# Attention stage of a streaming encoder: the low parts of the gated weights, subtracted on POOL for every unit

## What is computed

```
u = rms_norm(h, g_mix);  z = u @ w_in
q, k, v, a, b = split(z)               # 8 heads x 64; a and b are 512 wide
glu = a * sigmoid(b)                   # "gated" columns: the last 1024 of w_in
att = band_attend(rms_norm(q), rms_norm(k), v, rel_bias)   # own chunk of 64 and 8 before it
cv  = silu(layer_norm(depthwise_conv31(glu) + conv_b))
h   = h + concat(att, cv) @ w_out      # then a SwiGLU block and a gated embedding
```

## Time and profile before

| what | before |
|---|---|
| median of 3 runs | 2595.4 us (2593.06 to 2597.45) |
| profiled execution | 2595.5 us; its span 2593.7 us, 1.8 us around it |
| granted TensorE clock, mean | 0.999 |
| busy share PE / DVE / ACT / POOL | 99% / 71% / 49% / 23% |
| chain that ended last | PE 83%, DVE 6%, DMA 5% |
| DMA | 677.12 MB, mean 261 GB/s |

### The profile page before, as it was taken

One profiled execution on the slowest core, in us unless ns is written; L12 is line 12 of the kernel. 1 busy time (PEld: TensorE's weight loads), 2 busy tenths in 40 slices (PEclk: granted clock), 3 DMA queues, 4 the chain that ended last, 5 costly groups with the idle time before them and its releaser, 6 DMA issues.

```text
span 2593.7 us, 39929 instructions
## 1 busy us (share of the span) xinstructions
PE 2571.5 (99%) x13924; PEld 2497.0 (96%) x13924; DVE 1853.9 (71%) x3393; ACT 1266.1 (49%) x2283; POOL 597.2 (23%) x663
## 2 busy tenths in 40 slices
PE   9999999999999999999999999999999999999999
PEld 8999998999989999999999999999999999999999
DVE  4555579988888888777766877789538766666557
ACT  5344368888864323444334443423446443443465
POOL 6222211121121333323233333233200010111000
PEclk9999999999999999999999999999999999999999
DMA  5667798888677888898888898898896565665675
GB/s 204 215 214 244 237 361 272 280 290 273 201 242 250 289 302 282 303 349 286 307 320 312 281 335 300 303 325 314 294 348 190 162 188 183 187 197 181 198 238 186
DMA packets 316883, 677.12 MB, mean 261 GB/s; under 512 B 37485, under 2 KB 174573, under 8 KB 316141
## 3 DMA queue, kind: packets, MB, share of 16 engines
q1 hardware_dynamic: 295324, 603.78, 69.8%
q0 software_dynamic: 21360, 70.80, 7.7%
HBM read 512.19 MB, written 164.29 MB: 261 GB/s over the span
## 4 chain that ended last, share of the span: by engine, by line
PE 83%; DVE 6%; DMA 5%; ACT 2%; issue 2%; SPq 1%; POOL 0%; DVEq 0%; ACTq 0%; POOLq 0%
PE psum L198 51%; PE psum L2571 24%; PE psum L1556 2%; PE psum L1581 2%; DMA x<-in_w_gu 2%; PE psum L1543 1%; PE psum L1544 1%; DVE wres L3136 1%; DMA a_cr<-in_cache 1%; DVE y L3183 1%; DMA x<-in_w_down 1%; ACT wres L3004 1%; DVE ul L685 0%; POOL wres L628 0%; DMA rstd<-in_w_in 0%
## 5 line engine op out<-in xcount | busy, mean ns | idle before, releaser
L198 PE MATMUL psum<-uh,wres 128*128 128x416 f32 x3936 | 1119.2, 356 | 6.4 <-DVE wres L3136 2.6
L198 PEld LDWEIGHTS psum<-uh,wres 128*128 128x128 f32 x3936 | 736.8, 188 | 20.7 <-DVE wres L3136 5.7
L198 PE MATMUL psum<-ul,wres 128*128 128x416 f32 x1968 | 688.0, 350 | 0.0
L3004 ACT ACTIVATE wres<-x 128x1024 fp32r<-128x1024 f32 (+2 forms) x234 | 268.6, 1148 | 640.6 <-PE psum L198 536.2
L198 PE MATMUL psum<-wres 128*128 128x416 f32 x2304 | 447.9, 352 | 2.2 <-DVE wres L3136 2.2
L198 PEld LDWEIGHTS psum<-wres 128*128 128x128 f32 x2304 | 430.3, 188 | 9.9 <-DVE wres L3136 3.6
L2571 PE MATMUL psum<-wres 128*128 128x416 f32 x2104 | 426.0, 351 | 0.7 <-DVE c_top L2490 0.6
L2571 PEld LDWEIGHTS psum<-wres 128*128 128x128 f32 x2104 | 393.3, 188 | 6.3 <-issue 1.6
L198 PEld LDWEIGHTS psum<-ul,wres 128*128 128x128 f32 x1968 | 370.4, 188 | 6.6 <-issue 1.4
L3183 DVE SCALAR_TENSOR_TENSOR y<-c_top,vec,y 128x416 f32<-128x416 f32 (+1 forms) x600 | 339.2, 633 | 0.8
L1737 ACT ACTIVATE wres<-c_top 128x512 fp32r<-128x512 f32 (+1 forms) x302 | 181.3, 602 | 127.2 <-PE psum L2571 46.8
(11 more groups left out here) (314 smaller groups left out, 3628.0 us busy)
## 6 DMA issues: line engine op xcount, KB each, us to landing
x<-in_w_gu SPq DMA_DIRECT2D x132, 512.0 KB, 5.3
wres<-w_gu_lo SPq DMA_DIRECT2D x88, 512.0 KB, 6.1
c_top<-w_gu_sums SPq DMA_DIRECT2D x136, 256.0 KB, 3.2
x<-in_w_down SPq DMA_DIRECT2D x48, 704.0 KB, 6.6
w_gu_sums<-c_top POOLq DMA_DIRECT2D x60, 512.0 KB, 6.2
w_gu_lo<-wres SPq DMA_DIRECT2D x44, 512.0 KB, 6.4
c_top<-in_w_gu POOLq DMA_DIRECT2D x88, 256.0 KB, 5.8
wres<-w_down_lo SPq DMA_DIRECT2D x32, 704.0 KB, 7.5
```

The lines of the kernel that those rows point to most:

```text
L198: mm = nc.tensor.matmul(out, w[wp](kw), u[up](ku), start=first and n == 0 and j == 0, stop=last and n == len(kts) - 1 and j == 2)
L3004: nc.scalar.activation(whi[v % 2][:, 0:kts, :], raw[v % 2][:, 0:kts, :], ACT.Copy).then_inc(hi_done, 1)
```

## The change

All low parts of gated weights are made on POOL, by the same subtraction; none is stored and none loaded. In words: `weight_low` leaves DVE and stands in POOL's program, where each step now has its pair sums and, behind them, `weight_low(v + 2)` for the unit that ended one step before (the same step in which ACT makes the high part). `low_store`, `low_load` and the HBM tensor are gone. Every wait on a landing of a low part becomes a wait on the count of low parts (`lo_done`), and the raw places are held until POOL has read them: `weights(v)` always waits for `lo_done`, and so do the first raw loads of `finish`. The counts passed to `finish` follow.

```diff
--- before.py
+++ after.py
@@ -68,7 +68,7 @@
             "v2": dram("v2_d", (NT, HEADS * P), F32),
             "uh": dram("uh_d", ((NB - 1) * P, KD * N), F32), "ul": dram("ul_d", ((NB - 1) * P, KD * N), F32),
             "mh": dram("mh_d", (2 * AW, NT), F32), "ml": dram("ml_d", (2 * AW, NT), F32),
-            "w_glu": dram("w_glu_lo", (8 * P, D), F32), "w_out": dram("w_out_lo", (D, D), F32), "w_gu": dram("w_gu_lo", (2 * FF, D), F32),
+            "w_out": dram("w_out_lo", (D, D), F32), "w_gu": dram("w_gu_lo", (2 * FF, D), F32),
             "w_down": dram("w_down_lo", (D, FF), F32), "w_ple": dram("w_ple_lo", (D, D + PLE), F32),
             "w_s": dram("w_gu_sums", (4 * (FF + 12 * P), KH * P), F32),
         }
@@ -95,8 +95,8 @@
             project(nc, t, c, s)
             attend(nc, t, c, s, {"w_in": each, "hi_done": QKV + 6, "lo_done": QKV + 6, "used": NB * QKV + 4})
         GLUS = 8 * (NB - 1) + 2
-        finish(nc, t, c, s, {"w_in": each + 16 * GLUS // 2, "hi_done": QKV + 6 + GLUS, "lo_done": QKV + 14,
-                             "used": NB * QKV + 6 + GLUS, "low_dma": [16 * GLUS // 2] * 2 + [0] * 2})
+        finish(nc, t, c, s, {"w_in": each + 16 * GLUS // 2, "hi_done": QKV + 6 + GLUS, "lo_done": QKV + 6 + GLUS,
+                             "used": NB * QKV + 6 + GLUS, "low_dma": [0] * 4})
 
 
 def places(c):
@@ -970,7 +970,6 @@
         c["att_done"] = att_done
         w_in, hi_done, lo_done, used, u_read = c["w_in"], c["hi_done"], c["lo_done"], c["used"], sem("u_read")
         W0, H0, L0, U0 = base["w_in"], base["hi_done"], base["lo_done"], base["used"]
-        low_dma, OWN = c["low_dma"], 10
         u_in = [sem(f"u_in{k}") for k in range(NX)]
         z_out, tanh_out, glu_out = sem("z_out"), sem("tanh_out"), sem("glu_out")
         st_g = c["st_g"]
@@ -1080,25 +1079,10 @@
                              s["v2"][SEQ:NT, cols]).then_inc(cache_in, 16)
 
             def weights(v):
-                if v >= OWN + 2:
-                    sp.wait_ge(hi_done, H0 + v - 3)
-                else:
-                    sp.wait_ge(lo_done, L0 + v - 3)
+                sp.wait_ge(lo_done, L0 + v - 3)
                 m = QKV + (v + 8 - HELD) % 8
                 sp.dma_start(w_raw[:, v % 2, :, :].rearrange("p k c -> p (k c)"),
                              t["w_in"][m * P:(m + 1) * P, :]).then_inc(w_in[v % 2], 16)
-
-            def low_load(v):
-                sp.wait_ge(used, U0 + v - 1)
-                sp.wait_ge(low_dma[v % 2], 16 * (v // 2 - 1))
-                r = (v - 2) % 8
-                sp.dma_start(w_lo[:, v % 2, :, :].rearrange("p k c -> p (k c)").bitcast(F32),
-                             s["w_glu"][r * P:(r + 1) * P, :]).then_inc(low_dma[v % 2], 16)
-
-            def low_store(v):
-                sp.wait_ge(lo_done, L0 + v - 1)
-                sp.dma_start(s["w_glu"][(v - 2) * P:(v - 1) * P, :],
-                             w_lo[:, v % 2, :, :].rearrange("p k c -> p (k c)").bitcast(F32)).then_inc(low_dma[v % 2], 16)
 
             def first_raw(pair):
                 u = {"kind": "X", "pair": pair}
@@ -1179,9 +1163,6 @@
                 for b, k in reads_done(i - 1):
                     if k < NEXT:
                         u_load((b - 1) * KD + k + NX)
-                for v in units_done(i - 1):
-                    if OWN <= v + 2 < NV:
-                        low_load(v + 2)
                 for b, k in reads_done(i - LATER):
                     if k >= NEXT and b + 1 < NB:
                         u_load((b - 1) * KD + k + NX)
@@ -1199,18 +1180,16 @@
                     if v % 2:
                         glu_store(v // 2)
                 for v in units_done(i - 3):
-                    if v + 2 < OWN:
-                        low_store(v + 2)
                     if v + 4 < NV:
                         weights(v + 4)
                     elif v + 4 < NV + 2:
-                        sp.wait_ge(hi_done, H0 + v + 1)
+                        sp.wait_ge(lo_done, L0 + v + 1)
                         first_raw(v + 4 - NV)
             for pair in (2, 3):
                 if pair == 2:
                     sp.wait_ge(c["first_split"], 2)
                 else:
-                    sp.wait_ge(lo_done, L0 + OWN - 1)
+                    sp.wait_ge(lo_done, L0 + NV - 1)
                 u = {"kind": "X", "pair": pair}
                 sp.dma_start(unit_tiles(c["f_raw"][pair % 2], u, KD), unit_rows(t, u)).then_inc(w_in[pair % 2], 16)
             store(NP - 2)
@@ -1305,24 +1284,12 @@
                 dve.wait_ge(tanh_out, p + 1)
                 nc.vector.scalar_tensor_tensor(a, b, 1.0, a, ALU.add, ALU.mult).then_inc(glu_out, 1)
 
-            def weight_low(v):
-                dve.wait_ge(hi_done, H0 + v - 1)
-                if v >= 4:
-                    dve.wait_ge(low_dma[v % 2], 16 * (v // 2 - 1))
-                nc.vector.tensor_tensor(w_lo[:, v % 2, :, :], w_raw[:, v % 2, :, :], w_hi[:, v % 2, :, :].bitcast(F32),
-                                        ALU.subtract).then_inc(lo_done, 1)
-
             def gated(i):
                 for v in units_done(i - 3):
                     if v % 2:
                         gate(v // 2)
-                for v in units_done(i - 2):
-                    if v and v + 2 < OWN:
-                        weight_low(v + 2)
                 for v in units_done(i - 1):
                     evict(v)
-                    if v == 0:
-                        weight_low(2)
 
             def tap(n):
                 k, ct = TAP_ORDER[n]
@@ -1403,12 +1370,22 @@
                 nc.gpsimd.tensor_tensor(osum[:, k, 0, 0:wd], osum[:, k, 0, 0:wd], osum[:, k, 1, 0:wd],
                                         ALU.add).then_inc(osum_done, 1)
 
-            for n in range(NP):
-                if n == NP - 1:
-                    pool.wait_ge(hi_done, H0 + NV - 1)
-                    nc.gpsimd.tensor_tensor(c["f_lo"][1][:, 0:KD, :], c["f_raw"][1][:, 0:KD, :],
-                                            c["f_hi"][1][:, 0:KD, :].bitcast(F32), ALU.subtract).then_inc(lo_done, 1)
-                out_sum(n)
+            def weight_low(v):
+                pool.wait_ge(hi_done, H0 + v - 1)
+                nc.gpsimd.tensor_tensor(w_lo[:, v % 2, :, :], w_raw[:, v % 2, :, :], w_hi[:, v % 2, :, :].bitcast(F32),
+                                        ALU.subtract).then_inc(lo_done, 1)
+
+            for i in range(NU):
+                n = us[i]["n"]
+                if i == unit0[n] and n >= 3 and n % 2:
+                    out_sum(n // 2 - 1)
+                for v in units_done(i - 1):
+                    if v + 2 < NV:
+                        weight_low(v + 2)
+            pool.wait_ge(hi_done, H0 + NV - 1)
+            nc.gpsimd.tensor_tensor(c["f_lo"][1][:, 0:KD, :], c["f_raw"][1][:, 0:KD, :],
+                                    c["f_hi"][1][:, 0:KD, :].bitcast(F32), ALU.subtract).then_inc(lo_done, 1)
+            out_sum(NP - 1)
             pool.wait_ge(ath_done, NP)
             k = (NP - 1) % 2
             nc.gpsimd.tensor_tensor(atl[:, k, 0:DEC], att[:, k, 0:DEC], ath[:, k, 0:DEC].bitcast(F32),
@@ -1590,11 +1567,8 @@
                 if k == 0:
                     if v < 2:
                         pe.wait_ge(lo_done, L0)
-                    elif v < OWN:
+                    else:
                         pe.wait_ge(lo_done, L0 + v - 1)
-                    else:
-                        pe.wait_ge(hi_done, H0 + v - 1)
-                        pe.wait_ge(low_dma[v % 2], 16 * (v // 2))
                     if v >= 2:
                         pe.wait_ge(z_out, v - 1)
                     else:
```

## The result

The changed kernel takes 2612.01 us at the median of six runs (2608.69 to 2616.18), the one before, run beside it, 2594.65 (2592.46 to 2597.45). The ratio is 1.006, 95% interval 1.0049 to 1.0071: slower by 17.4 us by the medians, where 9.1 were forecast. The profiled execution took 2612.62, its span is 2610.9 against 2593.7.

The account below looks back on a forecast made before the run. PE, busy 99% of the span, was taken as the bound, DVE nearest to becoming it. Blocked taps lose 13.0 us, gains are 3.9: +9.1 on 2595.5 gives 2604.6 us, range 2596 to 2618.

Parts of the forecast that it names:

- The bound and the link: Attention stage: PE busy 99% bounds; PE's transposes wait for DVE's low parts L1263, 3.9 us in eight waits.
- Part 1: Subtraction moves from DVE to POOL: part ready in time, DVE's 9.7 us worth nothing beyond 0.7 gained in early units.
- Part 2: POOL's 2.41 us subtraction blocks DVE taps with two SBUF inputs until it ends, delaying L1263 and PE: 13.0 us lost.
- a hit: A unit whose DVE tap falls inside POOL's subtraction; 16 units, PE waiting 0.80 or 0.83 us in each.
- quiet units: Ten units at 438 to 539 us: tap starts 0.08 us before ScalarE's high part ends; no loss, except one at a turn.
- rival (b): Quiet units turn: POOL starts before the tap, transposes wait 2.1 us in six of ten; +12, 2617 us; chance 0.14.
- Part 3: 26 loads and eight stores go: PE's 1.89 us wait before 653.24 and the slow clock after it, 3.2 us gained.
- Part 4: Waits moved on SP and POOL: raw loads wait for POOL's low part, pair sums stand behind it; taken as 0.
- (c): Blocks stay but are absorbed as engines shift after one wait: half of 13 us, 2598, no measurable difference; chance 0.17.
- (d): Not slower: the hold misses so long an instruction or DVE's idle time takes it whole; 4.8 us gained, 2590.7; chance 0.11.

Follow-up runs that it names:

- two-part version: The changed kernel with POOL's subtraction cut into two instructions of half the tile: 2598.3 us, ratio 1.0012 to the kernel before.

## Why the prediction was right, and where its sizes were off

**The bound and the link** were right: PE lost its time waiting for L1242 (21.4 us), the next largest growth was 1.0 us, for POOL's first part. The size was not: 9.1 us were forecast and 17.4 measured, inside the range and nearly twice the forecast. The mis-sized terms are named below.

**Part 1** (the part comes in time, the move itself costs nothing) held. At the first unit PE waited 1.0 us at 352.7 for POOL's part of 2.38 us, but two waits for L1263 there had been 0.88 and 0.83 and one of 0.33 is left, so unit 2 took 0.3 less: "taken as 0" was near enough. PE's waits in units 5 to 7 fell from 0.4 to 0.2, as forecast. DVE's 9.7 us, worth nothing beyond 0.7 by the forecast, came out better: units 2 to 9 gained 1.6 together.

**Part 2** was right in mechanism and named the right instruction. The hold ended 0.45 after POOL (0.44 forecast), the next L1242 began 0.37 after it. The Trainium skill (SBUF — State Buffer, section on a bandwidth-pool intuition that's wrong) gives the end of the other instruction and some 115 ns for a DMA that a DVE copy holds up; the prediction carried that over to a tap. It doesn't fit there: the 46 stretched taps of this kernel, 0.65 us each when free, end 0.44 to 0.45 after POOL, not 0.76.

Two readings in this part were too wide. Seven taps L1337 were stretched before, not eight: the eighth instruction is L1333, the first tap of a channel tile, at 425.31. And L1333, a `tensor_scalar` in float32, reads only one SBUF tensor besides the columns of factors that every tap reads. It took 1.27 us there inside POOL's sum, and 0.49 elsewhere; so two SBUF inputs are not the only form that is held:

```profile
425.31 1.27 DVE L1333 TENSOR_SCALAR y<-b_gw,vec 128x416 f32<-128x416 f32 x1
...
425.04 1.30 POOL L1400 TENSOR_TENSOR b_osum<-b_osum,b_vlow 128x512 f32<-128x512 f32 x1 [9.88 <-ACT b_vlow L1456]
```

One mis-sized term is what a hit costs PE in the steady units: 0.80 and 0.83 were forecast, 1.02 and 1.06 a unit measured. Two small steps were left out of the sum. POOL starts 0.07 after ScalarE's end (597.01 against 596.94), and PE starts 0.15 after L1242's end (600.49 against 600.34), while the forecast let PE start at that end: 0.80 + 0.07 + 0.15 = 1.02, the measured value. In the nine steady units that is 2 us.

The larger miss is at the turns of head pairs. Units 19 to 21, forecast at 2.4, lost 5.2. The timeline of the changed kernel there shows that POOL's instruction in unit 19 met L1265, and PE waited 1.85 us behind that; in units 20 and 21 it met a tap, and PE waited 1.6 and 1.2 behind those, more than in a steady unit:

```profile
547.71 2.39 POOL L1375 TENSOR_TENSOR wres<-x,wres 128x1024 fp32r<-128x1024 f32 x1 [1.93 <-ACT wres L1445]
...
548.08 2.30 DVE L1265 TENSOR_TENSOR wres<-b_att,wres 128x256 fp32r<-128x256 f32 x1
...
559.81 2.37 DVE L1304 SCALAR_TENSOR_TENSOR y<-b_gw,vec,y 128x416 f32<-128x416 f32 x1
```

Only taps were counted as victims; L1265 is of the same kind and was overlooked. It was hit only this once. Units 26 and 27 (1.6 forecast, 2.6 measured) were hit at taps, with PE waits of 1.0 and 1.3 behind them. Unit 10 lost 0.95, also at a tap; the forecast had one hit of 0.8 at a turn among the quiet units. Why a held tap costs more at a turn is not shown; the units there are shorter.

**The quiet units** stayed quiet: rival (b), 2 us in six of them, didn't happen, though units 13, 15 and 17 lost 0.3 each to a tap held by a pair sum. The two-part version shows that the margin was thin: there the same three lost 0.9 to 1.1 each.

**Part 3** forecast a gain of 3.2 at the late load. Taking the loads from the kernel before gave 4.6 in units 28 and 29, taking them in the kernels without taps 5.2; in the changed kernel 2.0 are left of it, since each unit there pays its own hold (PE waits of 1.8 and 1.2; one hit of 0.83 was forecast for the two). The wait in unit 28, for activations loaded in the same burst (1.05 us in the kernel before, 1.21 in the run without taps), had been taken as 0.

**Part 4** (waits of SP, POOL's order) was right at 0 as far as the steady units show it: without the taps they take 11.61 to 11.66 us in the changed kernel too. POOL's order was not free elsewhere, since its sums, too, hold taps.

**Sum.** Forecast 13.0 lost and 3.9 gained, 9.1 net. Measured in the units: 0.95 + 1.1 + 5.2 + 4.1 + 2.6 + 5.3 = 19.3 lost, 1.6 and 2.0 gained, 15.7 net. The 6.6 between them are 2.0 in the nine steady units, 2.8 in units 19 to 21, 1.0 in 26 and 27, 1.1 in the quiet ones, 0.2 in unit 10 and 0.4 at the late load, less 0.9 more gained early.

"Absorbed" (c) and "not slower" (d) assumed more slack in DVE's order than there is. A hold of 1.71 us (a tap of 2.36 in place of 0.65) cost PE 1.02 in a steady unit, so some 0.7 was absorbed there, and later units were not spared by the shift of the first: all nine paid 1.0 to 1.1.

What stays open: how much of the 17 us is a shortage of DVE time and how much the place of the hold in its order. Moving POOL's part behind the tap gives units 22 to 25 all of their time back, halving it gives it back to all steady units, while DVE is 99% busy by the profile; no run takes DVE's time away without touching a hold.

## What to carry to other kernels

An idle POOL is not free when DVE has instructions that read two SBUF tensors: ask, for each long POOL instruction, which such DVE instruction will meet it (the taps here, and L1265), and what on PE waits for whatever stands behind that one in DVE's queue. If the work must go to POOL, cut it into shorter instructions: the held instruction gets in at the next boundary. Here four parts of 0.74 us were best, not one of 2.41 or two of 1.30, whose holds still cost, nor eight of 0.46, which end later for PE. A DVE busy share that rises while its work falls was the mark of such holds here; compare the mean of a line of fixed shape.

## What the runs showed of the hardware

The same bytes subtracted by POOL in one, two, four or eight instructions took a median of 2.41, 1.30, 0.74 and 0.46 us each. A line through the first two is 0.276 us per k-tile of 128 elements a partition and 0.20 fixed, which gives 0.75 and 0.47 for the others. So by the medians four parts cost POOL some 0.6 us a unit more and eight 1.3.

The hold goes both ways: a POOL sum of 1.3 us took 2.20 when it began under DVE's subtraction of two SBUF tensors. DVE's instructions that read PSUM for one input kept their time under a running POOL instruction everywhere in the stage of the changed kernel: L1242 (128x384) took 0.54 to 0.56 us, the evictions L1277 and L1280 0.57 to 0.59. A first tap with one SBUF tensor as input was held like the others (1.27 us before the change, 1.36 and 1.27 after, 0.49 free).
